# mLSTM heads, z tiles and half of the down projection in one order, with buffers moved and modulation loads sent earlier

## The reference: what is computed

```python
mx = jnp.split((jax.nn.silu(c) @ w_mod[layer] + b_mod[layer])[:, None, :], N_MOD, axis=-1)
...
xm, z = jnp.split(h @ w_up, 2, axis=-1)
xc = jax.nn.silu(dwconv_centred(xm, conv_w, conv_b))
q, k, v = blockdiag(xc, wq), blockdiag(xc, wk), blockdiag(xm, wv)
gates = sum(...) + b_if
h_f, st_f = mlstm_scan(qh, kh, vh, log_i[0], log_f[0], init[0])
h_b, st_b = mlstm_scan(flip_seq(qh), ...)
hs = layernorm_nobias(h_f + flip_seq(h_b), mh_norm)
return (hs + skip * xc) * jax.nn.silu(z), (st_f, st_b)
...
x = x + mx[2] * (from_colmajor(fx) @ w_down)
```

## Time and profile before

| | us |
|---|---|
| median of three runs (2678.19 to 2680.68) | 2678.35 |
| the profiled execution | 2677.56 |
| its span | 2675.6 |
| TensorE busy | 2396.7 |
| VectorE busy | 1437.2 |
| POOL busy | 1093.0 |
| ScalarE busy | 642.8 |

### The profile page before, as it was taken

The page is one execution under the profiler, slowest core; times in us unless marked ns, Lnnn a source line. Parts: engine busy times, 40 slices in busy tenths (PEclk is TensorE's granted clock), DMA queues, the critical chain, the costliest instruction groups (busy, mean ns, idle before and its releaser), DMA issues.

```text
span 2675.6 us, 33188 instructions
## 1 busy us (share of the span) xinstructions
PE 2396.7 (90%) x11971; PEld 1881.6 (70%) x11971; DVE 1437.2 (54%) x2474; ACT 642.8 (24%) x1044; POOL 1093.0 (41%) x822
## 2 busy tenths in 40 slices
PE   6899999998566989999999989998877978899998
PEld 2787888887323868888888868875435536688886
DVE  3584587674677347877787456541454254311113
ACT  2202345342675131000000142122221211300001
POOL 2353344332473424454354434463000304566663
PEclk9899999999877989999999989999888989899998
DMA  6563243343431244334343223344112112233332
GB/s 240 169 207 96 92 142 93 106 163 120 146 89 30 63 72 117 108 113 125 102 134 110 64 74 121 118 145 152 48 61 91 57 32 66 71 98 95 94 92 73
DMA packets 387508, 280.34 MB, mean 105 GB/s; under 512 B 30818, under 2 KB 350748, under 8 KB 387388
## 3 DMA queue, kind: packets, MB, share of 16 engines
q1 hardware_dynamic: 333452, 201.22, 25.9%
q10 hardware_dynamic: 53936, 77.51, 8.4%
HBM read 236.91 MB, written 41.78 MB: 104 GB/s over the span
## 4 chain that ended last, share of the span: by engine, by line
PE 57%; DVE 6%; ACT 2%; issue 1%; DMA 1%; ACTq 1%; POOL 0%; DVEq 0%; SPq 0%; POOLq 0%
PE PS L817 46%; PE PS L1345 3%; PE PS L1315 2%; PE PS L1291 1%; PE PS L762 1%; PE PS L768 1%; PE PS L1278 1%; ACT nh L1423 1%; PE PS L826 1%; DVE xcr L2065 0%; DVE mtmp L2533 0%; PE PS L1327 0%; PE PS L1203 0%; DMA xmr<-xm_d 0%; DVE mf_acc L1967 0%
## 5 line engine op out<-in xcount | busy, mean ns | idle before, releaser
L656 POOL TENSOR_TENSOR w_hi<-w_raw,ones 128x128 fp32r<-128x128 f32 x244 | 159.6, 654 | 1282.2 <-DMA w_raw<-in_ffn_w 451.9
L817 PE MATMUL PS<-act_hi,w_hi 128*128 128x512 f32 (+1 forms) x2080 | 642.9, 367 | 37.7 <-DVE act_lo L2024 18.0
L817 PE MATMUL PS<-act_hi,w_lo 128*128 128x512 f32 (+1 forms) x2080 | 624.0, 358 | 0.0
L817 PE MATMUL PS<-act_lo,w_hi 128*128 128x512 f32 (+1 forms) x2080 | 622.6, 357 | 0.0
L659 POOL TENSOR_TENSOR w_lo<-w_raw,w_hi 128x1024 fp32r<-128x1024 f32 (+1 forms) x244 | 589.2, 2415 | 20.4
L817 PEld LDWEIGHTS PS<-act_hi,w_hi 128*128 128x128 f32 x2080 | 346.1, 192 | 100.6 <-issue 35.3
L817 PEld LDWEIGHTS PS<-act_lo,w_hi 128*128 128x128 f32 x2080 | 344.9, 192 | 58.4 <-issue 0.5
L817 PEld LDWEIGHTS PS<-act_hi,w_lo 128*128 128x128 f32 x2080 | 344.1, 191 | 57.9
L1967 DVE SCALAR_TENSOR_TENSOR mf_acc<-mf_ring,cs,mf_acc 128x128 f32<-128x128 f32 x784 | 273.9, 424 | 2.0
L657 POOL TENSOR_SCALAR w_hi<-w_raw 128x896 fp32r<-128x896 f32 (+1 forms) x244 | 247.0, 1012 | 0.0
L2246 DVE SCALAR_TENSOR_TENSOR xT<-PS,modv,xT 128x512 f32<-128x512 f32 (+1 forms) x120 | 75.0, 658 | 275.0 <-PE PS L817 275.0
(11 more groups left out here) (328 smaller groups left out, 3193.6 us busy)
## 6 DMA issues: line engine op xcount, KB each, us to landing
w_raw<-in_ffn_w SPq DMA_DIRECT2D x120, 512.0 KB, 4.1
mf_ring<-in_w_mod SPq DMA_DIRECT2D x56, 512.0 KB, 4.0
w_raw<-in_a_w_in SPq DMA_DIRECT2D x44, 512.0 KB, 4.1
proj<-stage ACTq DMA_DIRECT2D x44, 384.0 KB, 3.9
w_raw<-in_b_w_up SPq DMA_DIRECT2D x32, 512.0 KB, 4.7
m_ring<-in_w_mod SPq DMA_DIRECT2D x12, 1024.0 KB, 8.4
rows<-g_d SPq DMA_DIRECT2D x16, 768.0 KB, 5.1
m_raw<-in_w_mod SPq DMA_DIRECT2D x4, 2048.0 KB, 17.1
```

Of the source, the lines that this page charges most:

```text
L656: pool.tensor_tensor(w_hi[:, s, 0], w_raw[:, s, 0], ones[:], ALU.mult)
L817: last = pe.matmul(to[:, c0:c1], w[:, s, k, :], x[:, k, c0:c1], start=k == 0 and w is w_hi and x is hi, stop=k == kt - 1 and w is w_lo)
```

## The change

It has three parts.

1. **One stage for heads, z and mout0.** Wb gets memory of its own, zs moves into the unused columns of xT, the gate rows move to other places, and act1_hi and act1_lo are gone: heads 1 and 2 write their outputs over columns 0 to 511 of act_hi and act_lo, heads 0 and 3 into the columns 512 to 767, in strips of 256 (head_act). Only z0 to z4 are done before the heads. z5 and z6 are laid into head 0's query and value, z7 and z8 into its scores, z9 to z15 into heads 0 and 1 before the denominators and before the spread rows; mout0's tiles take the same places in heads 2 and 3, and two more stand at the end of head 3. Evacuations on ScalarE (z_unit) and VectorE (first_out), the masks on POOL and the bank of each tile follow. The tile order of SP and POOL is as before.
2. **xs and zs** are loaded two tiles at a time (load_output).
3. **Modulation loads.** The first four m_ring loads stand ahead of the weights of qkv tile 4, later ones two tiles ahead; the first two mf_ring loads stand in up00's first ring of weights.

The core of the diff:

```diff
+        Wb = sb("Wb", [P, 6, LAT])
...
-        mr_i = sb("mr_i", [8, T], offset=0)
...
+        mr_i = rdiag[0:8, :]
+        mr_f = sb("mr_f", [8, T], offset=38912)
+        mr_ab = sb("mr_ab", [8, T], offset=41984)
+        mr_M = sb("mr_M", [8, 2, T], offset=38912)
+        mr_b = sb("mr_b", [8, 2, T], offset=45056)
+        mr_u = sb("mr_u", [8, 2, T], offset=51200)
+        mr_m = mr_b[:, :, 0:LAT]
...
-        act1_hi = nc.alloc_sbuf_tensor_at("act1_hi", [P, KD, LAT], F32R, offset=act_hi_at)
-        act1_lo = nc.alloc_sbuf_tensor_at("act1_lo", [P, KD, LAT], F32R, offset=act_hi_at + KD * LAT * 4)
-        Wb = nc.alloc_sbuf_tensor_at("Wb", [P, 6, LAT], F32, offset=act_hi_at + 2 * KD * LAT * 4)
-        zs = nc.alloc_sbuf_tensor_at("zs", [P, 2, LAT], F32, offset=act_hi_at + 2 * KD * LAT * 4 + 6 * LAT * 4)
...
+        def zs(i):
+
+            return xT[:, 2 * i + 4:2 * i + 6, LAT:T]
...
+        def in_strips(h):
+
+            return h in (0, 3)
+
+        def head_act(x, h, t):
+
+            return x[:, 2 * t:2 * t + 2, LAT:T] if in_strips(h) else x[:, 4 * (h - 1) + t, 0:LAT]
+
+        Z_BANK = (2, 0, 2, 0, 1, 6, 7, 6, 7, 6, 7, 6, 7, 6, 7, 6)
+        M_BANK = (6, 7, 6, 6, 7, 6, 2, 3)
...
-                    def load_both(r, s):
-                        load(r, s)
-                        if not (isinstance(r, int) and r == 1):
-                            sp.wait_ge(m_step, (r * RING + (s - 2 * RING + 1)) * (2 * KD))
-                        col = r * (2 * RING * P) + ((2 * s + 8) * P)
-                        sp.dma_start(m_ring[:, s], wmods[0][:, :, bass.ds(col, 2 * P)]).then_inc(m_in[s], 16)
-
-                    for s in range(RING):
-                        load_both(1, s)
-                    each_ring(sp, 2 * RING, 2 * RING, load_both)
+                    def load_columns(n):
+                        if n >= 2 * RING:
+                            sp.wait_ge(m_step, (n - 2 * RING + 1) * (2 * KD))
+                        col = (2 * n + 8) * P
+                        sp.dma_start(m_ring[:, n % RING], wmods[0][:, :, col:col + 2 * P]).then_inc(m_in[n % RING], 16)
+
+                    for n in range(RING, 2 * RING):
+                        load_columns(n)
+                    for n in range(RING, 4 * RING):
+                        load(n // RING, n % RING)
+                        if 2 * RING <= n + 2 < 4 * RING:
+                            load_columns(n + 2)
...
-                            if not (first and s < 2):
-                                sp.wait_ge(mf_step, (r * RING + (s - LATE0 - 1)) * (2 * KD))
+                            if first and s < 2:
+                                return
+                            sp.wait_ge(mf_step, (r * RING + (s - LATE0 - 1)) * (2 * KD))
...
-                        each_ring(sp, n0, RING, load)
+                        for s in range(RING):
+                            load(n0 // RING, s)
+                            if s == 1:
+                                for i in range(2):
+                                    col = (MOD_LATE + i) * P
+                                    sp.dma_start(mf_ring[:, i], wmods[0][:, :, col:col + P]).then_inc(mf_in[i], 16)
...
-                if name in ("mout0", "mout1"):
-
-                    each_ring(pool, n0, RING, lambda r, s: split(r, s, kt))
-                    for h in range(3) if name == "mout0" else (3,):
-                        for d in range(2):
...
-                    each_ring(pool, n0 + RING, count - RING, lambda r, s: split(r, s, kt))
+                def masks(h):
+                    for d in range(2):
+                        pool.wait_ge(de_done, DE_DONE0 + 2 * h + d + 1)
...
+                if name == "zm":
+                    for j in range(count):
+                        if j == 11:
+                            masks(0)
+                        split((n0 + j) // RING, j % RING, kt)
+                    continue
+                if name == "mout0":
+                    for m in range(count):
+                        if m in (1, 4, 7):
+                            masks((m + 2) // 3)
+                        split((n0 + m) // RING, m % RING, kt)
...
+            def z_steps(j, k0, k1):
+
+                if k0 == 0:
+                    pe.wait_ge(w_split, n0 + j + 1)
+                    if j in (13, 14):
+                        pe.wait_ge(fin_done, FIN_DONE0 + 4)
+                    else:
+                        pe.wait_ge(evac, n0 + j - 1)
+                    if j in (5, 6):
+                        pe.wait_ge(gr_put, 4)
+                for k in range(k0, k1):
+                    for w, x in ((w_hi, act_hi), (w_hi, act_lo), (w_lo, act_hi)):
+                        last = pe.matmul(bank(Z_BANK[j]), w[:, j % RING, k, :], x[:, k, 0:LAT],
...
+            def head_products(to, s, k, h, t):
+
+                out = halves(to) if in_strips(h) else to
+                for w, x in ((w_hi, act_hi), (w_hi, act_lo), (w_lo, act_hi)):
+                    last = pe.matmul(out, w[:, s, k, :], head_act(x, h, t),
...
+            def first_out_tile(m):
+
+                n = segs["mout0"][0] + m
+                pe.wait_ge(w_split, n + 1)
+                if m in (0, 1):
+                    pe.wait_ge(act_ready, READY["ml0"] + 8)
+                if m in (3, 4):
+                    pe.wait_ge(fin_done, FIN_DONE0 + 12)
+                elif m in (2, 5):
+                    pe.wait_ge(evac, n - 1)
+                elif m >= 6:
+                    pe.wait_ge(s6_put, S6_PUT0 + 24)
                 for k in range(KD):
-                    last = tile_products(j % RING, k, KD, act_hi, act_lo, LAT, 1 - j % 2)
+                    last = head_products(bank(M_BANK[m]), m % RING, k, k // 4, k % 4)
...
-            z_tile(3)
...
-            for j in range(4, 13):
-                z_tile(j)
-            pe.wait_ge(gm_done, 1)
-            pe.wait_ge(ge_done, 2)
...
-            for j in range(13, 16):
-                z_tile(j)
-            pe.wait_ge(evac, segs["mout0"][0])
+            z_tile(3)
+            z_tile(4)
...
+            def gate_columns():
+
+                pe.wait_ge(gm_done, 1)
+                pe.wait_ge(ge_done, 2)
+                pe.wait_ge(evac, n0 + 5)
...
+                last.then_inc(gc_mm, 1)
...
+                    if h == 0:
+                        z_steps(5, 2 * t, 2 * t + 2)
...
+                        if h == 0:
+                            z_steps(6, f - 4, f - 3)
...
             query(0)
             value(0)
+            scores_of(0, (0, 1))
+            gate_columns()
+            scores_of(0, (2,))
             stabiliser_rows(0)
-            scores_of(0, range(6))
+            scores_of(0, (3,))
+            z_tile(7)
+            z_tile(8)
+            scores_of(0, (4, 5))
             for h in range(ML_HEADS):
 
+                if h == 0:
+                    z_tile(9)
+                    z_tile(10)
+                    z_tile(11)
+                elif h == 1:
+                    z_tile(13)
+                    z_tile(14)
+                elif h == 2:
+                    first_out_tile(0)
+                    first_out_tile(1)
+                else:
+                    first_out_tile(3)
+                    first_out_tile(4)
                 pe.wait_ge(den_rdy, DEN_RDY0 + h + 1)
                 for d in range(2):
                     for c in range(4):
                         last = pe.matmul(bank(0)[:, 4 * d + c:4 * d + c + 1], mtmp[:, 1 + d, c * P:c * P + P], ones[:, 0:1], start=True, stop=True)
                 last.then_inc(den_mm, 1)
+                if h < 2:
+                    z_tile(12 + 3 * h)
+                else:
+                    first_out_tile(3 * h - 4)
                 pe.wait_ge(rd_rdy, RD_RDY0 + h + 1)
-                if h == 2:
-
-                    project("mout0", act1_hi, act1_lo, LAT, act_ready, READY["ml0"])
-                    pe.wait_ge(evac, segs["mout1"][0])
                 pe.matmul(bank(0), ones[:], rdiag[:, 0:LAT], start=True, stop=True)
                 pe.matmul(bank(1), ones[:], mtmp[:, 0], start=True, stop=True).then_inc(rfb_mm, 1)
                 if h + 1 < ML_HEADS:
                     query(h + 1)
 
...
-                if h:
-                    pe.wait_ge(fin_done, FIN_DONE0 + 4 * h)
+                pe.wait_ge(evac, (n0 + 13, n0 + 16, n0 + 19, n0 + 22)[h])
...
                 if h + 1 < ML_HEADS:
                     stabiliser_rows(h + 1)
                     value(h + 1)
+                else:
+                    first_out_tile(6)
 
                 pe.wait_ge(hs_rdy, HS_RDY0 + h + 1)
                 pe.matmul(bank(7), ones[:], mtmp[:, 1], start=True, stop=True).then_inc(mean_mm, 1)
 
                 if h + 1 < ML_HEADS:
                     scores_of(h + 1, (0, 1))
+                else:
+                    first_out_tile(7)
...
-            project("mout1", act1_hi, act1_lo, LAT, act_ready, READY["ml1"], together=3)
+            n0 = segs["mout1"][0]
+            for s in range(3):
...
```

(75 more changed lines are left out.)

79 lines of the change are left out of this document (43 added, 36 removed).

## The result

The changed kernel takes 2598.44 us (median of four runs, 2593.81 to 2604.72) against 2678.38 us for the kernel before beside it: a ratio of 0.9692, 95% interval 0.9678 to 0.9706, 80 us less. The profiled execution is the quickest of the four, 2593.81 us, 83.75 less than the profiled one of before.

The account below looks back on a forecast made before the run. TensorE was taken as the busiest engine, losing time in the heads to idle stretches (82.2 of 466.8 us) and a slow clock. 77 (stage) + 15 (qkv) + 1 (up00) = 93 off 2677.56 gives 2585 us; range 2573 to 2610.

Parts of the forecast that it names:

- the forecast one: The case in which the prediction's own sum holds, 2585 us; chance 0.75.
- The merged stage: From z tile 2 to the second half of the down projection: 77 us less, by moving 19 z and out tiles.
- The five stretches: Stage cut at the ends of the heads' scores: savings of 47.5, minus 14.5, 0.5, 45.5, minus 0.4; sum 78.6 us.
- The predicted idle before the denominators: Sign of being right: TensorE idle under 2 us before L1327 in heads 1 to 3, denominators taking 2.0 us.
- value's wait: In value of the next head: the 4.65 us wait stays, three times, with its slow clock.
- POOL against VectorE: Splits now fall between VectorE's head operations: 1 us a head for heads 1 to 3, ends 0 and 6.6.
- Rival (a): Heads 1 to 3: three splits each delay VectorE, 6.6 us not 1, plus 3 half clock; 2614 us; chance 0.12.
- (c): The only rival in which the kernel becomes slower; its further wording is not in the text; chance 0.03.
- The modulation loads: In qkv, early m_ring loads save 15 us, ends 12 and 18.
- 13.0 for tile 4: In qkv, tile 4 took from 102.3 to 124.7 and should take 9.4 us like the next three: 13.0 saved.
- Later weight loads stand behind a column load ..., so nothing: In qkv: the column load waits for a unit two tiles back, up to 9.4 us; cost to later weights nothing.
- up00: The 6.7 us wait for mf_acc stays, put down to ScalarE's table DMAs; moving mf_ring loads gives 1 us, ends 0 and 3.

Follow-up runs that it names:

- e2: The changed kernel with the m_ring and mf_ring loads back where they stood before, so the merged stage alone; 2604.4 us, ratio 0.9714.
- e1: The changed kernel run once more, unaltered; 2599.23 us, ratio 0.9701.
- e4: The changed kernel, but in qkv POOL splits tile n (from 8 on) only after VectorE's modulation unit n - 2; 2595.54 us, ratio 0.9684.
- e5: The changed kernel, but from qkv tile 8 on each column load goes with its own tile's weights; 2596.58 us, ratio 0.9694.
- e8: The changed kernel, but ScalarE issues the 13 small table loads behind the ffn's up stages; 2596.89 us, ratio 0.9695.
- e9: The changed kernel, but in up00 VectorE makes the first late modulation products (mf_acc) before its hidden tiles; 2591.31 us, ratio 0.9671.
- e12: The changed kernel with e5's column loads, e9's products first and e8's table loads together; 2588.93 us, ratio 0.9661.
- e10: The changed kernel, but z12 and z15 stand before the denominators of heads 0 and 1, not between them and the spread rows; 2615.22 us, ratio 0.9755.
- e11: e5, but POOL writes the low halves of qkv tiles 8 to 15 as zeros with a one-input operation, omitting part of the result; 2590.04 us, one run.
- e6: The changed kernel, but ScalarE copies head h+1's value tiles before making that head's weights; 2601.9 us, ratio 0.9714.
- e7: The changed kernel, but ScalarE makes the next head's weights behind the root, VectorE's first two weighted scores follow the first finished tile; 2594.58 us, ratio 0.9694.

## Why the prediction was right, and where it was not

The forecast was 2585 us with a range of 2573 to 2610; 2598.44 lies in it, and the case was the forecast one. It asked for 93 us and 80 came.

**The merged stage: right.** 77 us were predicted and 78.0 found in the first trace, 76.2 in e2 by its time. The other traces in which the stage is unaltered (e1, e2, e4, e5, e8, e9, e12) have it at 390.2 to 392.4 us, 74 to 77 less than before. The five stretches:

| stretch | predicted | measured |
|---|---|---|
| to head 0's scores | 69.3 | 68.8 |
| to head 1's | 88.7 | 88.4 |
| to head 2's | 84.7 | 84.1 |
| to head 3's | 84.8 | 84.7 |
| to the second half | 60.7 | 62.8 |

The stretches are the recorded sums, without the 1.6 us taken off for changes between kinds of product, an estimate with no row behind it; in the first trace that was not needed. The last stretch took 2.1 more, of which 1.6 are out5 at part of the clock. The predicted idle before the denominators (under 2 us) and their 2.0 us are there, and value's wait stayed. What e10 adds is that the split of the tiles between the two gaps matters: two tiles misplaced cost about a fifth of the whole gain.

**POOL against VectorE.** I took 1 us a head, though the terms of 84.8 leave it out for head 2. TensorE paid 0.1 us for it at 1929.42 and waited 0.2 at L1414 in head 3; more does not show before the spread rows of heads 1 to 3, where the long operation at 1925.71 lies under z15. In the qkv stage, where I had counted one split a unit (9.4 us) and not two, the same cost makes units uneven: 8.65 us beside a split and 5.63 without one (e4, e11). A product took 2.61 us beside a POOL instruction of 2.44 (e5), and 1.26 beside one of 1.10 (e11). Rival (a), three splits a head that each catch a VectorE operation, did not come. The 3 us of half clock a head in its sum are shown by no run; behind value's wait it was 2.5 us, 5.73 for 24 instructions of which 12 take 1.60 at full clock.

**Slower,** (c), to which 0.03 was given, did not come either: the granted clock was 0.96 to 1.00 in all five stretches. It was still low behind value's wait: 0.50 through the 5.7 us behind the wait of 4.65 before, and 0.52 through 5.5 us behind the wait of 4.79 now.

**The modulation loads: the step that failed.** I wrote 15 us for qkv, from 13.0 for tile 4, 1.1 for its split wait and 1 for smaller waits; 7.2 came by the end of the modulation, and 5.2 to 7.7 in time. Tile 4 gave 11.2, not 13.0 (22.4 us before, 11.2 now, since it began partly at half clock behind its wait). That split wait grew by 1.0 instead of going: the slot is free only at 90.3, and the load, now issued together with two other weight loads, took 8.8 us until POOL began (99.04), where it took 7.5 with a column load beside it. The rest is the sentence that "Later weight loads stand behind a column load ..., so nothing". That was costed by the mean rate of units. The queue holds the weights for every second tile back, two splits then fall into one unit, and that unit is late: 3.4 us were lost again between tile 4 and the end, where 1 was to be gained. So of the 7.9 us that are missing, 3.5 are missing at tile 4 and 4.4 behind it. e5 takes the second part out: behind tile 4 it gains 1.1 us, as forecast, and its modulation ends 11.0 us ahead of before. What keeps it from 15 is tile 4, which ends 9.9 us ahead and not 14; rd's split costs no more than it did before (3.05 us against 2.97).

**up00: the number right, the reason wrong.** The wait stayed (7.11 us against 6.71), as predicted. But it was put down to ScalarE's 18.5 us of issuing table loads; e8 took them away and 5.3 us stayed. VectorE's own order held it (e9: 1.2 us are left). The 1 us for moving the first two mf_ring loads does not show in the wait either. Had I asked what stood ahead of the first product on VectorE, not who ended its last idle time, the row would have shown it.

**What is left open.** From the end of the modulation to z tile 2 the kernels of e4, e5, e6, e7 and e10 are the changed kernel, and yet this stretch takes 1521.7 to 1525.3 us in their traces; runs of the changed kernel differ by 11 us. Why the loads gave 7.2 us at 229 and 5.2 to 7.7 in time can't be told more closely than that.

## What to carry to other kernels

A stage in which TensorE waits for short chains on other engines can be filled by cutting independent work to the size of each gap. Here the sum of such an edit, made from single rows, came out within 2.1 us a stretch; the place of each tile is part of the edit. A load that is allowed to wait on a queue holds back the loads issued behind it (weights left 2.3 and 3.6 us late here): ask for each wait what the next issue is, not what the mean rate is. And before a wait on the chain is counted as a gain, follow the other outputs of the engine that ends it: the 14.4 us of waits in value were taken away twice, and both times 11.6 us of other waits came in.

## What the runs showed of the hardware that was not expected

POOL and VectorE slowed each other. In e11 a 128x128 operation on POOL took 2.61 us instead of 0.50, at 129.92, while VectorE's products ran on at 0.48 us each; it ended 0.33 us behind the last of them, at 132.53. In four more splits beside a unit it took 2.81 to 2.94 us. And a POOL operation that reads only one tile of SBUF slowed VectorE as well: a product took 1.26 us beside one of 1.10, where most take 0.48.

The granted clock fell with hardly any idle time: behind a wait of 0.17 us and the 16 one-column sums of the denominators (1.95 us), out5 ran with a granted clock of 0.50 from about 2093 to 2096 and took 7.17 us instead of 5.56. It did so in e1, e2, e5, e6, e8, e9 and e12 too: 7.16 to 7.21 us behind waits of 0.17 to 0.94, with 0.52 to 0.62 granted in the second to fourth us of the tile. In e7, where the sums took 1.68 us and not 1.95, it took 5.56 at a granted clock of 1.00, and so did the tiles behind the same sums in heads 0 and 2 (5.55 or 5.56). But in head 1 the sums took 1.95 or 1.96 as well, and the tile behind them 5.6 (7.22 in e6), and in e10's head 3 a wait of 0.99 us and sums of 1.95 were followed by a tile of 5.56. What decides it no run here shows.
